# Attention step of a two-layer macaron decoder: the values' products of the older pair issued ahead of the next pair's transposes

## What is computed

```
x = x + 0.5 * swiglu(rms_norm(x), ffn1)                 # D_FF = 2816
z = rms_norm(x) @ w_in                                  # split into q, k, v, indexer q/k/w, pool, memory q
y = concat(dsa_attention(q, k, v, indexer),             # 8 heads x 64, causal, top 128 keys per query
           multiscale_pool(pool),                       # 4 groups x 64, windows 2/4/8/16
           memory_attention(mem q, mem))                # 4 heads x 64 into 256 memory tokens
x = x + y @ w_out
x = x + 0.5 * swiglu(rms_norm(x), ffn2)
```

## Time and profile before

| what | value |
|---|---|
| runs, median | 1928.07 us (1926.75 to 1928.64, 3 runs) |
| the profiled execution | 1927.92 us, its span 1926.1 us |
| busy in the span: PE, ACT, DVE, POOL | 99%, 50%, 32%, 18% |
| mean granted clock of TensorE | 0.999 |
| attention's steps n = 0 to 46, layer 0 | 500.62 to 562.41 us of the span |

### The profile page before, as it was taken

How to read it: one execution, slowest core, us unless ns; L and a number is a source line. 1 busy time by engine, 2 the same in 40 slices (tenths; PEclk the granted TensorE clock), 3 DMA queues, 4 the chain that set the end, 5 groups by cost and what they waited for, 6 DMA issues and landing times.

```text
span 1926.1 us, 25986 instructions
## 1 busy us (share of the span) xinstructions
PE 1904.4 (99%) x9100; PEld 1546.9 (80%) x9100; DVE 616.9 (32%) x1181; ACT 958.7 (50%) x1294; POOL 349.2 (18%) x397
## 2 busy tenths in 40 slices
PE   7999999999999999999999999999999999999999
PEld 5888888877768888888888888888877788888887
DVE  5222210268753322220052222003786442222101
ACT  5444443565665544443364444335657564444432
POOL 1111111112511111111111111111226011111110
PEclk9999999999999999999999999999999999999999
DMA  7988888778237888888878888888791379888885
GB/s 209 215 193 190 193 194 192 185 191 189 81 89 175 207 191 199 186 190 195 194 184 197 201 186 193 195 195 192 183 209 40 86 181 228 196 186 198 187 194 140
DMA packets 96105, 348.15 MB, mean 181 GB/s; under 512 B 10800, under 2 KB 11056, under 8 KB 95792
## 3 DMA queue, kind: packets, MB, share of 16 engines
q0 software_dynamic: 46512, 169.37, 49.3%
q1 hardware_dynamic: 48960, 175.67, 28.3%
q10 hardware_dynamic: 576, 2.36, 0.3%
HBM read 175.91 MB, written 2.10 MB: 92 GB/s over the span
## 4 chain that ended last, share of the span: by engine, by line
PE 95%; DVE 2%; DMA 2%; ACT 1%; issue 1%; SPq 0%; DVEq 0%; ACTq 0%; POOLq 0%
PE bank L507 93%; PE bank L881 1%; DMA w_lo<-raw 1%; DVE h_lo L1212 0%; DMA raw<-weights 0%; DVE x L1235 0%; DVE t L1440 0%; DVE pt L358 0%; DVE r L1225 0%; ACT w_lo L989 0%; ACT prob L1151 0%; ACT w_hi L988 0%; ACT t L1151 0%; ACT a_hi L1167 0%; PE bank L664 0%
## 5 line engine op out<-in xcount | busy, mean ns | idle before, releaser
L988 ACT ACTIVATE w_hi<-raw 128x1024 fp32r<-128x1024 f32 x323 | 342.1, 1059 | 834.5 <-PE bank L507 799.8
L507 PE MATMUL bank<-h_hi,w_hi 128*128 128x512 f32 x1648 | 647.5, 393 | 12.1 <-ACT h_hi L967 9.0
L507 PE MATMUL bank<-h_hi,w_lo 128*128 128x512 f32 x1648 | 642.6, 390 | 0.0
L507 PE MATMUL bank<-h_lo,w_hi 128*128 128x512 f32 x1648 | 627.1, 389 | 0.2 <-DVE h_lo L1212 0.2
L418 POOL DMA_DIRECT2D w_lo<-raw x323 | 279.0, 869 | 1502.8 <-ACT w_lo L989 1465.9
L507 PEld LDWEIGHTS bank<-h_hi,w_hi 128*128 128x128 f32 x1648 | 310.1, 188 | 85.7 <-issue 17.7
L507 PEld LDWEIGHTS bank<-h_lo,w_hi 128*128 128x128 f32 x1648 | 309.3, 188 | 65.8 <-issue 1.4
L507 PEld LDWEIGHTS bank<-h_hi,w_lo 128*128 128x128 f32 x1648 | 310.2, 188 | 64.5
L989 ACT ACTIVATE w_lo<-raw 128x1024 fp32r<-128x1024 f32 x323 | 336.7, 1042 | 0.0
L507 PE MATMUL bank<-a_hi,w_hi 128*128 (+1 forms) x832 | 324.6, 390 | 0.0
L507 PE MATMUL bank<-a_lo,w_hi 128*128 (+1 forms) x832 | 323.8, 389 | 0.0
(11 more groups left out here) (149 smaller groups left out, 1134.8 us busy)
## 6 DMA issues: line engine op xcount, KB each, us to landing
raw<-weights SPq DMA_DIRECT2D x326, 512.0 KB, 4.6
w_lo<-raw POOLq DMA_DIRECT2D x323, 512.0 KB, 5.8
x<-x_t SPq DMA_DIRECT2D x4, 512.0 KB, 7.9
mem<-mem_t ACTq DMA_DIRECT2D x2, 1024.0 KB, 7.0
out_t<-x SPq DMA_DIRECT2D x8, 256.0 KB, 2.1
const<-consts SPq DMA_DIRECT2D x1, 481.5 KB, 9.8
wpool<-pool_w ACTq DMA_DIRECT2D x2, 128.0 KB, 7.0
par<-params SPq DMA_DIRECT2D x1, 38.0 KB, 3.5
```

Source lines behind the costliest of these rows:

```text
L507: return nc.tensor.matmul(out_, lhsT, rhs, start=start, stop=stop, skip_group_check=True)
L988: nc.scalar.activation(w_hi[:, s], raw[:, s], ACT.Copy).then_inc(w_hi_done, 1)
```

## The change

In PE's list of attention, `times_v` of the pair n - 6 is issued ahead of the transposes of units n - 4 and n - 3. Nothing else is changed: the same instructions, the same waits in front of each, the same lists on ACT, DVE, POOL and SP.

```diff
                     if n - 2 in group_after:
                         spread_sums(group_after[n - 2])
+                    if 0 <= n - LAG - 2 < UNITS:
+                        times_v(n - LAG - 2)
                     if 0 <= n - LAG < UNITS:
                         transpose_p(n - LAG)
                         transpose_p(n - LAG + 1)
-                    if 0 <= n - LAG - 2 < UNITS:
-                        times_v(n - LAG - 2)
                     for b in FILL.get(n, ()):
                         fill(b)
```

## The result

The changed kernel took **1932.8 us** (median of 16 runs, 1930.8 to 1941.3) against 1926.6 for the kernel before (16 runs beside it, 1925.0 to 1931.0). The ratio is 1.0031 with a 95% interval of 1.0023 to 1.0039: slower, by about 6 us where 9 were forecast.

The account below looks back on a forecast made before the run. PE was taken to bound the kernel, so only its waits count. Carried stalls made each of 2 layers 4.5 us later, +9.0 on the profiled 1927.9; with the median 0.15 above, 1937 us, range 1931.5 to 1941.5.

Parts of the forecast that it names:

- the old five stalls: PE's five waits a layer, before the change, for DVE's copy of an odd unit ahead of a transpose: 2.5 us.
- Rival D: DVE's group sums come up to 1.0 us earlier and all ten old stalls go: 5.1 us less, 1922.8; chance 0.05.
- Rival C: PE's wait only changes place, since DVE starts copies earlier: within 3 us of before, 1929; chance 0.09.
- Rival B: ACT's 8.2 us of waiting for transposes absorbs the push, only (a) and (b) are paid: 1932.9; chance 0.16.
- (a): Only the logits cover the newest copy before the values' products: stalls of 0.05 us in plain 4-block steps, 0.39 step 8.
- (b): At the five old stalls, transposes that ran in front of the stall now run behind it: 1.5 us a layer.
- B's sign: What would show the forecast wrong in favour of Rival B: PE stalls in attention under 6 us in all.
- the split of step 18: DVE's split there, beside a POOL operation, was taken as 1.39 us; running free, 1.0 us a layer less.
- behind step 46: Output projection fills stand between transposes and values' products there, so nothing more is lost after 4.5 us of lateness.
- The sign of 1.8 us at step 18: The step of 3 blocks at 526.6 would begin some 1.8 us later.
- (c): Later transposes push ACT's copies, its exponentials and DVE's work, biting at ACT's weight rounding: stall of 1.59 us at step 16.
- rival E: PE stalls of 1.5 us, twice within 6 us, could lower the clock in attention: 10 us more, 1947; chance 0.04.

Follow-up runs that it names:

- e1: Changed order, but only one of the two transposed units goes behind the values' products: 1930.0 us, ratio 1.0010.
- e3: Old order with DVE's split_y one unit later, behind the odd copy: 1919.8 us, ratio 0.9962.
- e6: Changed order in all steps but step 6, which keeps the transposes ahead of the values' products: 1937.3 us in six runs.
- e2: Changed order with DVE's split_y one unit later, behind the odd copy: 1927.4 us, ratio 1.0000.
- e9: Changed order with ACT's four weight roundings at units 9, 17, 25, 33 instead of 9, 11, 21, 23: 1950.7 us, ratio 1.0109.
- e5: Old order without POOL's windowed sums, the pooling product taking the plain projection: 1925.4 us, ratio 0.9988.
- e10: Old order with DVE's later split, and the values' products first only from step 46 on: 1920.9 us, ratio 0.9950.
- e4: Changed order with three plain float32 matmuls ahead of the values' products of steps 16 and 28: 1938.9 us.

## Why the prediction was right, and where it was not

**Direction and mechanism: right.** No work was added, the wait for the odd copy moved from the transposes to the values' products, with more and longer stalls. e1 shows that the cover is what counts, e3 that the old five stalls were the split in front of the copy. Rival D (faster) is out: DVE's copy of unit 9 starts at 520.55 and its sums at 520.89, in the order of its list. Rival C is out by the ratio.

**Rival B has the number, and not the mechanism.** B said that ACT's slack takes the push up: only (a) and (b) are paid, 2.5 us a layer, 1932.9. Measured are 2.6 and 1932.8. But by B the copies would come when they came before. Against step 0 the copy of unit 11 came at 26.50 us, 24.96 before; step 18 began 1.90 us later in layer 0 and 2.0 in layer 1 (forecast 1.8), step 46 3.4 later; the stalls add up to 7.0 us a layer, where B's sign was under 6. ACT's waits for transposes doubled, and it was pushed all the same. The end came out at B's figure by luck: two gains that neither account had, the undisturbed split of step 18 and what comes back behind step 46, are told below.

**(a)** Steps 8 and 12 hold: 0.33 for 0.39 in step 8. Step 12 has 0.16 in layer 1 for 0.22. **Step 6 was missed.** I gave it 0.05; it is 0.58, since `times_v(0)` also waits (line 898) for DVE to have emptied the y bank of `u`, which the transposes had hidden. e6 shows what it is worth: 0.2 us a layer, for step 16, with a split that POOL holds up, gives the rest back. The sign of 1.8 us at step 18 came true in part by luck: the missed 0.6 us of step 6 made up for a split that took 0.69 us and not 1.0.

**(c)** The chain through ACT's rounding, the copy of 8, the exponentials of 12, DVE's maximum of 14 and the split is in the changed kernel's rows in that order. It bites one copy earlier than I had it: ACT waits 0.99 us for transposes ahead of the copy of unit 4 (at 514.09; 0.57 before) and has no gap from there to the exponentials of 12. Most stalls of layer 0 are near, the profile's own idle beside the forecast: step 26 0.76 for 0.7, step 28 1.24 for 1.2, step 36 0.28 for 0.35, step 40 0.63 for 0.65, step 44 0.61 for 0.55; step 16 has 1.18 for 1.59. **The term that failed** is the split of step 18: "At its new time, 530.9, POOL has its next operation running, so I take 1.39". It took 0.42 and 0.43 us in the two layers. Step 20's stall was 0.38 us and not 1.5, and between steps 18 and 22 PE gained 0.3 us where I had it lose 0.7: that 1.0 us is nearly all by which 4.5 missed the 3.4 that layer 1 shows at step 46.

The moment was reckoned rightly. The split did begin while POOL's next operation, L449, was running (527.53 to 529.06, the split 528.43 to 528.85, rows above), and neither was slowed. What failed is that I took the price of one POOL operation for another. L451 has two tensor inputs; beside it the same split took 1.39. L449 multiplies one tensor by a constant. In e2 a split that began 0.11 us behind the start of L449 took 1.10 for 0.69; in e6 one that began 0.63 behind it took 0.43. My estimate from these rows: L449 holds a split up for its first 0.5 us only. At the prediction's own time the split begins 0.66 us behind the start of L449 (530.24 in the kernel before), which is late enough. The page "SBUF — State Buffer" of the Trainium skill, section "SBUF: two separate sides", says that whichever of the two instructions starts first keeps the other out to its end. The rows of e1, e6 and e9 (1.75, 1.60 and 1.63 us beside L433, 0.69 without POOL's operations in e5) agree with it; the rows of L449 do not.

**Behind step 46** I had "nothing more is lost". In fact 0.8 us a layer comes back (2.6 at the end against 3.4). e10 shows it alone, on the old order (8.9 us behind step 46 against e3's 9.6).

**The clock, rival E (chance 0.04).** It came in as a part and not as the case: 1.3 us in layer 0 of the profiled execution, nothing in layer 1, and outliers up to 1941 us. So one of my signs of being wrong, slow matmuls in attention, did appear, in one of two layers. Its condition, stalls of 1.5 us, did not come in: the fall came with stalls of 0.76 and 1.24. The price of 10 us was too high for the changed kernel; for e9's order it is about right, by an estimate from its clock column (some 10 us at half clock in a layer, so 5 us of work lost, twice). I had also read the earlier trace rows as full clock everywhere, where a fall outside attention was hidden. The Trainium skill, page "TensorE: Matmul & The Clock Gate", Part 1, has the clock fall behind idleness; the rows of e9 agree, with 2.50 and 2.11 us of idle ahead of its two falls.

**The sum.** Of 9.0, 5.3 are measured in the loops (2 x 2.6). The other 3.7 are step 20's stall and its split (some 2), what came back behind step 46 (some 1.5) and small things. The medians differ by 6.2, executions at full clock by 5.4; that the 0.9 between 5.3 and 6.2 is falls of the clock is likely, but the runs do not settle it. The expected waits at L507 for DVE's copy were 12 to 15 us in 20 or more times; they are 9.8 in 17.

## What to carry to other kernels

When stations of a software pipeline run on three engines, the order on the busiest one decides how long the others have: moving a consumer ahead takes its own duration, and that of what it overtakes, from the cover of the newest handover. Before reordering the bound engine, look at what stands in front of the late instruction on the engine that makes it wait; here one line on DVE was worth 6 to 8 us and the order on PE cost 6. And a duration that was stretched by a neighbour belongs to its moment and to that neighbour's kind: after any shift, reckon with the one measured alone at the one end and the stretched one at the other.

## What the runs showed that was not expected

- A VectorE operation with two inputs in SBUF (128x256 and 128x512) took 0.42 and 0.69 us alone and up to 1.39 and 1.75 when it began beside a two-input operation of POOL (the kernel before, e1, e6, e9). When it began first, POOL's took longer instead: 1.77 us for 1.25 (e1). Beside POOL's multiplication by a constant it was held only near that one's start (e2), and not at 0.6 us or more behind it (the changed kernel, e6). A gain of 1.0 us on ACT was swallowed by this in e9, and most of the lead of e6.
- Stalls of PE of 2.1 to 2.5 us, several in one attention loop, were followed by a half clock for 3 to 7 us (e9). Its profiled execution took 13.9 us more than the changed kernel's, and the stalls in PE's rows add up to 8.2 more; the falls are the likely rest. Stalls of 0.8 to 1.2 brought it in some executions only.
- Three matmuls of 512 columns with plain float32 operands took 2.8 us (e4), while rounded ones start 0.23 us apart.
- The new order gives a little back. The values' products start 0.92 us behind the first matmul of the spreading of sums (514.97 to 515.89, changed kernel), the transposes in their old place 1.02 (516.43 to 517.45, before); in step 50 spreading, transposes and values' products take 1.44 us to the output's first matmul, 1.76 before. Why was not tried.
